# ScalarE's weight blocks in the attention steps: one ahead of the exponentials, the others at the end

## The chip, the cores and the metric

One core of a Trainium2 chip runs the whole program in one launch. The metric is the device time of a run in microseconds; of three runs of the kernel before, the median is 1616.29 us (1611.82 to 1618.34). PE is TensorE, PEld its weight load, DVE is VectorE, ACT ScalarE, POOL GpSimd, SP SyncE.

## What is computed

Three layers over 512 tokens of width 1024, in float32. Layer 0: windowed attention (8 heads, a window of 128, a learned sink) beside a multi-scale pooling, then an MLP. Layer 1: dense latent attention beside a gated recurrence, then an MLP. Layer 2: a short convolution, sparse attention with three branches (compressed, selected, window) and dilated attention with three dilations, then a gate. The two parts that the change touches compute, cut down:

```python
# layer 0 ("even")
s = where(|kpos - qpos| <= 128, q @ k.T * 64**-0.5, -inf)
m = maximum(max(s), sink); p = exp(s - m)
out = (p / (sum(p) + exp(sink - m))) @ v
x = x + concat([out, pooled(u)]) @ e_w_out
# layer 2 ("last")
u = rmsnorm(x) @ w_in_2          # 33 tiles of 128 columns
y_b = gate0 * softmax(q k_cmp) v_cmp + gate1 * softmax(q k_s) v_s + gate2 * softmax(q k_w) v_w
y_c = alpha_g * softmax(q k_dilated) v   # three groups
h = x + concat([y_a, y_b * silu(z), y_c * silu(z)]) @ w_out_2
```

## The kernel before

**Weights.** All weights come as one stream of 232 blocks, each 128x1024 (eight sub-blocks of 128x128). SP loads block b into slot b mod 4 of `raw`. The products are made with split numbers, three matmuls for one (L575, L576, L577): high by high, high by low, low by high. So each block is split on the chip: ACT copies it into its high half (`prepare`, L1048, in the MLPs L1143; semaphore `hi_made`), POOL subtracts to get the low half (L558, `lo_made`), and PE waits for `lo_made` before its first product with the block. `prepare(n)` makes all blocks up to n; for block b it waits for the load and for PE's last use of block b-4 (`acc_full` or `block_used`). POOL and SP run one loop over all blocks, each in the order of the stream.

**Attention.** Each of the three attentions (`attention("even", ...)`, `"mla"`, `"last"`) is a software pipeline over pairs of units (a unit is one head or branch on 128 queries). In step s PE makes the scores of pair s (L680), the values of pair s-3 (L698), the transposes of pair s-2 (L712), and then a fill: products of other work. DVE adds the mask and takes the minimum (L1555, out `negm`, semaphore `masked`), and scales the probabilities of pair s-1 (L1563, then L1569 or L1571, `p_ready`). ACT runs the exponentials of pair s (L1104) and copies the transposes of pair s-2 out of the bank (L1114, `pt_ready`). PE's scores of pair s+1 wait for `masked` of pair s, its values for `pt_ready`.

**Fills.** In the even attention (19 steps) the fill is four to six products a step of the remaining input tiles, the pooling map and the first part of the output map (`e_pace`, `E_BLOCKS`). In the last one (51 steps, numbered 0 to 50 here) it is the input projection: 12 products in steps 0 to 3, 10 in steps 4 to 11, then 4, from step 36 on 3 (`pace`, `Z_BLOCKS`). Some blocks of it are "parts" of the compression, used up by four matmuls at L946. DVE takes each finished tile out of its bank (L1886, L1884, in the even attention L1516, L1710, L1522) and runs what follows from it in `behind`, ahead of the next step's L1555: L1927 and L1932 (the dilated output by its share and by silu), L1861, L1624, L1628 (the short convolution), L1452 (low halves of the operands), in the even attention L1677 to L1692 (window sums) and L1530 to L1532 (rotations).

**ACT's order.** It is the order in which the code is written. In a step of the attentions:

```python
beside(step)              # copies and activations for tiles that the step before finished
exponentials(step)
turned_probs(step - 2)    # L1114
between(step)             # weight blocks
evacuate(k)               # at the end of a group
```

In the even and the last attention `between` makes the blocks whose slots the fill of the step before gave free; the one in the mla attention makes none. In the last attention steps 2 to 5, 8, 9 and 12 make two blocks, 6 and 7 three, 1, 10 and 11 one, and from step 14 on the steps 14, 16, ... 36 and 39, 42, 44 one each.

Of the kernel before, what the change touches and what calls it, by code (L numbers as in the profile page):

```python
# [37 lines left out]
RING = 4  # L38
# [202 lines left out]
def e_steps(n_steps):  # L241

    work, done, blocks, at = e_work(), [], [], 0
    ends = HEAD + E_AHEAD // SUBS
    for step in range(n_steps):
        events = []
        for stage, i, k in work[at:at + e_pace(step)]:
            count = {a: n for a, _, n in STAGES}[stage]
            sub = SUB0[stage] + i * count + k
            if k == count - 1:  # L250
                events.append((stage, i))
            ends += sub % SUBS == SUBS - 1 or (stage == "pool" and i == NTILES["pool"] - 1)
        at += e_pace(step)
        done.append(events)
        blocks.append(ends)
    assert at >= len(work), (at, len(work))
    return done, blocks
# [12 lines left out]
def z_steps(n_steps):  # L270

    work = [w for w in z_work(HEAD)] + [("out2", i, k) for i, k in OUT2_HEAD]
    done, blocks, at, ends = [], [], 0, HEAD
    for step in range(n_steps):
        names, left = [], pace(step)
        while at < len(work) and left:
            kind, n, what = work[at]
            at += 1
            if kind == "aside":
                names.append(what)  # L280
                continue
            left -= 1
            if kind == "product" and what == KT - 1:
                names.append(Z_HOSTS[n])
                ends += 1
            if kind == "part":
                ends += 1
                if what[1] == 3:
                    names.append(f"part{what[0]}")
        done.append(names)  # L290
        blocks.append(ends)
    assert at == len(work), (at, len(work))
    return done, blocks


def program(nc, x_t, stream, params, consts, ropes, p_t, out_t):
    with ExitStack() as ctx:
# [126 lines left out]
        E_DONE, E_BLOCKS = e_steps(len(EVEN) // 2 + VALUE_LAG)  # L424
# [16 lines left out]
        def z_banks():  # L441

            t0, held, out = TILE0["zin"], {}, {}
            for n in range(HEAD):
                out[Z_HOSTS[n]] = (4 + (t0 + n) % 4, None)
                held[4 + (t0 + n) % 4] = z_tile(Z_HOSTS[n])
            for n in range(HEAD, len(Z_HOSTS)):
                own, other = 6 + (n + 1) % 2, 6 + n % 2
                out[Z_HOSTS[n]] = (own, held.get(own))
                held[own] = z_tile(Z_HOSTS[n])  # L450
                for _, aside in Z_ASIDES.get(n, ()):
                    out[aside] = (other, held.get(other))
                    held[other] = z_tile(aside)
            return out, held
# [3 lines left out]
        Z_DONE, Z_BLOCKS = z_steps(len(LAST) // 2 + VALUE_LAG)  # L458
# [64 lines left out]
        def probs(i, n):  # L523

            return more[:, i % 4 - 2, 0:n] if i % 4 >= 2 else tmp[:, 2 + i % 4, 0:n]

        def groups_after(family, step):

            n = max(u["group"] for u in FAMILY[family]) + 1
            return [k for k in range(n) if last_of(family, k) // 2 + VALUE_LAG == step]  # L530
# [506 lines left out]
        def _(act):  # L1037
            prepared = [0]

            def prepare(n):  # L1040

                while prepared[0] <= min(n, NBLOCKS - 1):
                    b = prepared[0]
                    act.wait_ge(raw_in[b % RING], 16 * (b // RING + 1))
                    if b >= RING:
                        what, count = BLOCK_END[b - RING]
                        act.wait_ge(acc_full if what == "tile" else block_used, count)
                    nc.scalar.activation(w_hi[:, b % RING, :], raw[:, b % RING, :], ACT.Copy).then_inc(hi_made, 1)  # L1048
                    prepared[0] += 1
# [38 lines left out]
            def rows(stage):  # L1088
                return lambda m: act.wait_ge(z_ready, TILE0[stage] + m + 1)

            def attention(family, evacuate, beside=lambda step: None, between=lambda step: None):
                units, u0 = FAMILY[family], UNIT0[family]
                pairs = len(units) // 2

                def exponentials(p):
                    for i in (2 * p, 2 * p + 1):
                        u, gu = units[i], u0 + i
                        act.wait_ge(masked, gu + 1)
                        if u["sink"] is not None:
                            act.wait_ge(sink_put, gu + 1)  # L1100
                        if p >= 2:
                            act.wait_ge(pt_full, gu - 3)
                        w = u["n"] + (u["sink"] is not None)
                        nc.scalar.activation(probs(i, w), tmp[:, i % 2, 0:w], ACT.Exp, bias=negm[:, i:i + 1], scale=-1.0,  # L1104
                                             accum_out=den[:, i:i + 1]).then_inc(exp_done, 1)

                def turned_probs(p):
                    for i in (2 * p, 2 * p + 1):
                        u, gu = units[i], u0 + i
                        act.wait_ge(pt_full, gu + 1)  # L1110
                        if p:
                            act.wait_ge(pv_done, gu - 1)
                        w, m = (u["n"] + P - 1) // P * P, min(P, u["n"])
                        nc.scalar.activation(tmp[0:m, 4 + i % 2, 0:w], bank[4 + i % 2][0:m, 0:w],  # L1114
                                             ACT.Copy).then_inc(pt_ready, 1)

                for step in range(pairs + VALUE_LAG):
                    beside(step)
                    if step < pairs:
                        exponentials(step)  # L1120
                    if 0 <= step - TURN_LAG < pairs:
                        turned_probs(step - TURN_LAG)
                    between(step)
                    for k in groups_after(family, step):
                        evacuate(k)

# [92 lines left out]
                            act.wait_ge(z_ready, TILE0["pool"] + i + 1)  # L1219
                            hi_of("pooled", i, pooled_y[i])  # L1220

            def between_even(step):
                if step >= 1:
                    prepare(E_BLOCKS[step - 1] + RING - 1)

            def even_out(k):
                group_done("even", k)
                hi_of("eattn", k, bank[(GROUP0["even"] + k) % 2][:, :])

            attention("even", even_out, beside_even, between_even)  # L1230
            prepare(E_BLOCKS[-1] + RING - 1)
            act.dma_start(rope[:, :, :], ropes[1]).then_inc(rope_in, 16)

# [122 lines left out]
            block0 = SUB0["zin"] // SUBS  # L1356
# [43 lines left out]

            prepare(block0 + HEAD + RING - 1)

            def between_last(step):
                if step >= 1:
                    prepare(block0 + Z_BLOCKS[step - 1] + RING - 1)

            def last_out(k):
                if k >= 3:
# [2 lines left out]
                        act.wait_ge(acc_full, z_tile(1) + 1)  # L1411
                    hi_of(f"nsa{k - 3}", 0, z2(15 + k))

            attention("last", last_out, beside_last, between_last)
            act.wait_ge(p_in, 16)
            for k in range(2):
                nc.scalar.activation(mlp_op[:, 0, k, :], arena[:, 11 + k, :], ACT.Copy).then_inc(mlp_hi, 1)
# [747 lines left out]
```

## Time and profile before

| | |
|---|---|
| median of three runs | 1616.29 us (1611.82 to 1618.34) |
| the profiled execution | 1611.82 us, span 1610.0 us |
| mean granted clock of PE in it | 0.969 |
| PE busy | 1489.6 us, 93% |
| DVE, ACT, POOL busy | 783.1, 622.9, 566.1 us |
| even attention | about 44 to 161 us |
| last attention | about 1200 to 1509 us |

In the rows below a time is in us from the span's start. A row of a timeline has the start, the duration, the engine, the line, the operation, what it writes and reads, and how many alike were merged; in brackets stands how long the engine was idle before it and what ended that. A busy PE is not PE at its peak, since matmuls overlap. The granted clock is given as a share of 2.4 GHz.

### The profile page before, as it was taken

To read this page: it belongs to the slowest core of one execution; us is meant where nothing else is said; L and a number is where in the kernel's file an instruction comes from. 1 tells how busy PE (TensorE), PEld (TensorE's weight loads), DVE (VectorE), ACT (ScalarE), POOL (GpSimd) and SP (SyncE) were. 2 spreads that over 40 slices of the span, in tenths; PEclk is the share of its full clock that TensorE was granted. 3 is DMA by queue.
4 is the path that set the end of the run, shared out by engine and by line. 5 is a ranking of instruction groups with operands and counts; after the bars stand their busy time and mean duration, and the time that the engine had idled before them with its cause. 6 is when DMAs were issued, how large, how long until landed. Compare 5 with 4: busy or idle time off the path is not lost.

```text
span 1610.0 us, 20388 instructions
## 1 busy us (share of the span) xinstructions
PE 1489.6 (93%) x7110; PEld 1167.8 (73%) x7110; DVE 783.1 (49%) x1417; ACT 622.9 (39%) x1126; POOL 566.1 (35%) x236
## 2 busy tenths in 40 slices
PE   6979899999999987788999999999989799899997
PEld 5657678888888866545778888888867677666785
DVE  6783442223444677586333223444466236476434
ACT  4443332232323456545433232232353234655432
POOL 4222254444444433100235444444423352122441
PEclk9999999999999988979999999999989999899998
DMA  5212232322223221100123232332322232111221
GB/s 215 68 51 66 66 105 91 102 94 96 100 91 103 70 89 66 53 1 1 61 76 112 91 104 92 99 97 91 104 66 79 92 107 77 40 53 53 66 79 53
DMA packets 36624, 129.55 MB, mean 80 GB/s; under 512 B 4048, under 2 KB 4176, under 8 KB 36560
## 3 DMA queue, kind: packets, MB, share of 16 engines
q1 hardware_dynamic: 35136, 124.80, 23.7%
q10 hardware_dynamic: 1424, 3.90, 0.7%
q8 instruction: 40, 0.66, 0.2%
q14 instruction: 24, 0.20, 0.0%
HBM read 126.58 MB, written 2.10 MB: 80 GB/s over the span
## 4 chain that ended last, share of the span: by engine, by line
issue 58%; POOL 22%; PE 16%; DVE 2%; ACT 1%; POOLq 1%; DVEq 0%; ACTq 0%
POOL w L558 22%; PE bank L575 4%; PE bank L577 4%; PE bank L576 4%; PE bank L698 1%; PE bank L712 1%; PE bank L680 1%; DVE arena L1996 0%; POOLq L557 0%; POOLq L555 0%; ACT tmp L1114 0%; ACT tmp L1104 0%; DVE arena L1628 0%; DVE arena L1886 0%; ACT arena L1383 0%
## 5 line engine op out<-in xcount | busy, mean ns | idle before, releaser
L558 POOL TENSOR_TENSOR w<-raw,w 128x1024 fp32r<-128x1024 f32 x232 | 565.9, 2442 | 1010.8 <-ACT w L1048 628.2
L575 PE MATMUL bank<-opC,w 128*128 128x512 f32 x624 | 255.3, 409 | 26.0 <-POOL w L558 14.2
L577 PE MATMUL bank<-opC,w 128*128 128x512 f32 x624 | 246.8, 395 | 0.0
L576 PE MATMUL bank<-opC,w 128*128 128x512 f32 x624 | 246.4, 395 | 0.0
L1604 DVE TENSOR_TENSOR mlp_op<-arena,mlp_op 128x512 fp32r<-128x512 f32 x64 | 144.5, 2260 | 188.7 <-ACT mlp_op L1171 188.7
L575 PE MATMUL bank<-mlp_op,w 128*128 128x512 f32 x560 | 221.5, 396 | 10.0 <-DVE arena L1516 9.5
L1143 ACT ACTIVATE w<-raw 128x1024 fp32r<-128x1024 f32 x126 | 133.2, 1057 | 239.5 <-PE bank L577 239.5
L576 PE MATMUL bank<-mlp_op,w 128*128 128x512 f32 x560 | 220.5, 394 | 0.0
L577 PE MATMUL bank<-mlp_op,w 128*128 128x512 f32 x560 | 220.3, 393 | 0.0
L575 PE MATMUL bank<-opA,w 128*128 128x512 f32 x428 | 168.8, 394 | 6.8 <-ACT arena L1317 2.3
L577 PE MATMUL bank<-opA,w 128*128 128x512 f32 x428 | 167.4, 391 | 0.0
L576 PE MATMUL bank<-opA,w 128*128 128x512 f32 x428 | 167.2, 391 | 0.0
L575 PEld LDWEIGHTS bank<-opC,w 128*128 128x128 f32 x624 | 119.3, 191 | 55.9 <-issue 14.5
L1597 DVE TENSOR_TENSOR tmp<-tmp,rms 128x512 f32<-128x512 f32 x64 | 51.5, 805 | 210.9 <-ACT tmp L1151 210.5
L577 PEld LDWEIGHTS bank<-opC,w 128*128 128x128 f32 x624 | 119.0, 191 | 26.1
L576 PEld LDWEIGHTS bank<-opC,w 128*128 128x128 f32 x624 | 119.5, 191 | 23.0 <-issue 0.5
L575 PEld LDWEIGHTS bank<-mlp_op,w 128*128 128x128 f32 x560 | 106.7, 191 | 34.2 <-DVE arena L1516 11.0
L1151 ACT ACTIVATE tmp<-bank 128x512 f32<-128x512 f32 x64 | 38.3, 598 | 224.5 <-PE bank L577 213.9
L577 PEld LDWEIGHTS bank<-mlp_op,w 128*128 128x128 f32 x560 | 106.6, 190 | 22.5
L576 PEld LDWEIGHTS bank<-mlp_op,w 128*128 128x128 f32 x560 | 106.6, 190 | 22.2 <-issue 0.2
L1048 ACT ACTIVATE w<-raw 128x1024 fp32r<-128x1024 f32 x106 | 109.4, 1049 | 14.0 <-PE bank L577 13.2
L575 PEld LDWEIGHTS bank<-opA,w 128*128 128x128 f32 x428 | 80.6, 188 | 27.8 <-ACT arena L1317 5.6
(213 smaller groups left out, 1928.2 us busy)
## 6 DMA issues: line engine op xcount, KB each, us to landing
raw<-stream_dram SPq DMA_DIRECT2D x232, 512.0 KB, 3.4
out_t_dram<-arena SPq DMA_DIRECT2D x8, 256.0 KB, 2.1
x<-x_t_dram SPq DMA_DIRECT2D x4, 256.0 KB, 5.7
x<-x_t_dram ACTq DMA_DIRECT2D x4, 256.0 KB, 7.2
rope<-ropes_dram ACTq DMA_DIRECT2D x2, 512.0 KB, 6.8
con<-consts_dram ACTq DMA_DIRECT2D x1, 993.5 KB, 8.2
arena<-p_t_dram ACTq DMA_DIRECT2D x1, 512.0 KB, 4.2
par<-params_dram ACTq DMA_DIRECT2D x1, 253.5 KB, 3.8
```

The costliest lines, as they stand in the source:

```text
L558: pool.tensor_tensor(w_lo[:, j, :], raw[:, j, :], w_hi[:, j, :].bitcast(F32), ALU.subtract).then_inc(lo_made, 1)
L575: pe.matmul(out, wh, hi, start=first, stop=False)
L576: pe.matmul(out, wh, lo, start=False, stop=False)
L577: return pe.matmul(out, wl, hi, start=False, stop=last)
L680: pe.matmul(bank[2 + i % 2][:, 0:u["n"]], u["q"], u["k"], start=True, stop=True).then_inc(s_full, 1)
L698: mm = pe.matmul(into[at:at + 64, col:col + P], u["v"][b], tmp[0:kw, 4 + half, P * b:P * (b + 1)], start=(b == 0 and u.get("first", True)) ...
L712: mm = pe.transpose(bank[4 + i % 2][0:w, a:a + P], probs(i, SEQ)[:, a:a + w], ident)
L1048: nc.scalar.activation(w_hi[:, b % RING, :], raw[:, b % RING, :], ACT.Copy).then_inc(hi_made, 1)
L1143: nc.scalar.activation(w_hi[:, b % RING, :], raw[:, b % RING, :], ACT.Copy).then_inc(hi_made, 1)
L1151: nc.scalar.activation(tmp[:, j % 2, :], bank[4 + (t0 + j) % 4][:, :], ACT.Relu).then_inc(relu_made, 1)
L1597: TTn(tmp[:, j % 2, :], tmp[:, j % 2, :], rms[:, 1, :], ALU.mult).then_inc(vstep, 1)
L1604: TTn(mlp_op[:, 1, j % 2, :], u[:, bass.ds(SEQ * RING * i + SEQ * j, SEQ)], mlp_op[:, 0, j % 2, :].bitcast(F32), ALU.subtract).then_inc(ml ...
```

## The change

`attention` on ACT gets `blocks`, a function from the step to the number of the last block that may be made, in place of `between`. Ahead of the exponentials it makes blocks up to `min(blocks(step), prepared[0])`, which is one block if any is due; behind the copies it makes the rest. The functions of the two attentions return the numbers that they passed to `prepare` before; `-1` means none.

```diff
-            def attention(family, evacuate, beside=lambda step: None, between=lambda step: None):
+            def attention(family, evacuate, beside=lambda step: None, blocks=lambda step: -1):
...
                 for step in range(pairs + VALUE_LAG):
                     beside(step)
+                    prepare(min(blocks(step), prepared[0]))
                     if step < pairs:
                         exponentials(step)
                     if 0 <= step - TURN_LAG < pairs:
                         turned_probs(step - TURN_LAG)
-                    between(step)
+                    prepare(blocks(step))
                     for k in groups_after(family, step):
                         evacuate(k)
...
-            def between_even(step):
-                if step >= 1:
-                    prepare(E_BLOCKS[step - 1] + RING - 1)
+            def blocks_even(step):
+                return E_BLOCKS[step - 1] + RING - 1 if step else -1
...
-            def between_last(step):
-                if step >= 1:
-                    prepare(block0 + Z_BLOCKS[step - 1] + RING - 1)
+            def blocks_last(step):
+                return block0 + Z_BLOCKS[step - 1] + RING - 1 if step else -1
```

ACT in steps 5 and 6 of the last attention, before (w is a weight block's high half, raw_in the load of its slot, acc_full and block_used the release of the old block):

```order
L1048 ACTIVATE w<-raw 128x1024 [waits block_used,raw_in0]
L1104 ACTIVATE tmp,den<-tmp,negm 128x128 [waits pt_full,masked] x2
L1114 ACTIVATE tmp<-bank 128x128 [waits pv_done,pt_full] x2
L1048 ACTIVATE w<-raw 128x1024 [waits acc_full,raw_in1]
L1048 ACTIVATE w<-raw 128x1024 [waits acc_full,raw_in2]
L1048 ACTIVATE w<-raw 128x1024 [waits acc_full,raw_in3]
L1104 ACTIVATE more,den<-tmp,negm 128x128 [waits pt_full,masked] x2
```

and with the change:

```order
L1048 ACTIVATE w<-raw 128x1024 [waits block_used,raw_in0]
L1048 ACTIVATE w<-raw 128x1024 [waits acc_full,raw_in1]
L1104 ACTIVATE tmp,den<-tmp,negm 128x128 [waits pt_full,masked] x2
L1114 ACTIVATE tmp<-bank 128x128 [waits pv_done,pt_full] x2
L1048 ACTIVATE w<-raw 128x1024 [waits acc_full,raw_in2]
L1048 ACTIVATE w<-raw 128x1024 [waits acc_full,raw_in3]
L1048 ACTIVATE w<-raw 128x1024 [waits block_used,raw_in0]
L1104 ACTIVATE more,den<-tmp,negm 128x128 [waits pt_full,masked] x2
```

The first of step 6's three blocks (raw_in1) stands ahead of its exponentials, and the first of step 7's (raw_in0, the last but one row) ahead of step 7's.

ACT in step 24, before, from the Silu of six tiles on:

```order
L1383 ACTIVATE arena<-arena 128x512 [waits z_ready] x6
L1104 ACT_TABLE_LOAD [waits pt_full]
L1104 ACTIVATE tmp,den<-tmp,negm 128x31 [waits masked]
L1104 ACTIVATE tmp,den<-tmp,negm 128x31 [waits pt_full,masked]
L1114 ACTIVATE tmp<-bank 128x512 [waits pv_done,pt_full] x2
L1048 ACTIVATE w<-raw 128x1024 [waits acc_full,raw_in0]
```

and with the change:

```order
L1383 ACTIVATE arena<-arena 128x512 [waits z_ready] x6
L1048 ACTIVATE w<-raw 128x1024 [waits acc_full,raw_in0]
L1104 ACT_TABLE_LOAD [waits pt_full]
L1104 ACTIVATE tmp,den<-tmp,negm 128x31 [waits masked]
L1104 ACTIVATE tmp,den<-tmp,negm 128x31 [waits pt_full,masked]
L1114 ACTIVATE tmp<-bank 128x512 [waits pv_done,pt_full] x2
```

The step's only block moves from behind the copy of the transposes to ahead of the exponentials. The rows of PE, DVE, POOL and SP are the same in both kernels.

## Rows read from the trace of the kernel before

**Rows 1.** The page, busy time: us, share of the span, instructions.

```profile
PE 1489.6 (93%) x7110; PEld 1167.8 (73%) x7110; DVE 783.1 (49%) x1417; ACT 622.9 (39%) x1126; POOL 566.1 (35%) x236
```

**Rows 2.** PE's waits, 1195 to 1530: us in total, times, longest.

```profile
PE bank L575 <- POOL w L558: 12.2, 6, 4.3
PE bank L698 <- ACT tmp L1114: 10.3, 6, 7.3
...
PE bank L680 <- DVE negm L1555: 2.8, 3, 1.4
```

**Rows 3.** PE's waits, 44 to 172.

```profile
PE bank L575 <- DVE op_any L1452: 4.0, 2, 2.3
PE bank L680 <- DVE arena L1532: 2.7, 2, 2.2
```

**Rows 4.** Timeline of steps 5 and 6 of the last attention, PE, ACT, POOL.

```profile
1260.12 0.47 PE L575 MATMUL bank<-opC,w 128*128 128x512 f32 x1 [3.16 <-POOL w L558]
...
1268.27 0.40 ACT L1104 ACTIVATE tmp<-tmp,negm 128x128 f32<-128x128 f32 x1 [9.77 <-DVE negm L1555]
...
1270.49 6.99 POOL L558 TENSOR_TENSOR w<-raw,w 128x1024 fp32r<-128x1024 f32 x3 [8.09 <-ACT w L1048]
...
1272.99 0.76 PE L575 MATMUL bank<-opC,w 128*128 128x512 f32 x1 [4.26 <-POOL w L558]
```

**Rows 5.** Windows: us; busy PE, PEld, DVE, ACT, POOL; clock; DMA; GB/s.

```profile
1260.10:1263.10 3.00, 2.98 (x14) 2.47 (x15) 0.00 (x0) 0.00 (x0) 2.31 (x1) 1.00 0.50 175
1273.00:1278.70 5.70, 5.70 (x15) 4.54 (x16) 0.00 (x0) 0.00 (x0) 4.49 (x2) 0.50 0.61 192
1391.36:1401.60 10.24, 5.82 (x30) 5.01 (x31) 1.22 (x8) 7.24 (x17) 2.35 (x1) 0.50 0.13 31
```

**Rows 6.** Timeline, POOL and DVE, at 1369 and at 1487.

```profile
1369.46 2.39 POOL L558 TENSOR_TENSOR w<-raw,w 128x1024 fp32r<-128x1024 f32 x1 [9.01 <-ACT w L1048]
1369.86 2.60 DVE L1571 TENSOR_SCALAR tmp<-tmp,rden,gates 128x384 f32<-128x384 f32 x2
...
1487.00 0.87 DVE L1571 TENSOR_SCALAR more<-more,rden,gates 128x384 f32<-128x384 f32 x2
...
1489.14 3.38 POOL L558 TENSOR_TENSOR w<-raw,w 128x1024 fp32r<-128x1024 f32 x1 [8.34 <-ACT w L1048]
```

**Rows 7.** Timeline of step 28, DVE and PE's next scores.

```profile
1411.79 0.69 DVE L1886 TENSOR_TENSOR arena<-bank,rms 128x512 f32<-128x512 f32 x1 [0.68 <-PE bank L577]
1412.39 1.89 DVE L1932 TENSOR_TENSOR arena<-arena 128x512 f32<-128x512 f32 x3
...
1415.48 0.08 DVE L1555 DVE_READ_ACCUMULATOR2_ANT negm<- 128x1 f32 x1
...
1415.80 0.49 PE L680 MATMUL bank<-arena 64*128 64x256 f32 x2
```

**Rows 8.** Timeline of steps 26, 34 and 39, DVE and PE's next scores.

```profile
1404.02 1.89 DVE L1927 TENSOR_TENSOR arena<-arena 128x512 f32<-128x512 f32 x3
...
1438.71 0.69 DVE L1886 TENSOR_TENSOR arena<-bank,rms 128x512 f32<-128x512 f32 x1 [1.47 <-PE bank L577]
...
1440.17 0.55 DVE L1624 TENSOR_SCALAR arena<-arena,par 128x512 f32<-128x512 f32 x1
...
1445.49 0.70 PE L680 MATMUL bank<-arena 64*128 64x512 f32 x2 [1.38 <-DVE negm L1555]
...
1467.31 0.49 PE L680 MATMUL bank<-arena 64*128 64x256 f32 x2 [0.79 <-DVE negm L1555]
```

**Rows 9.** Timeline behind steps 24, 30 and 44, ACT and PE.

```profile
1395.62 1.05 ACT L1048 ACTIVATE w<-raw 128x1024 fp32r<-128x1024 f32 x1
...
1395.78 0.48 PE L698 MATMUL bank<-tmp,arena 128*64 128x128 f32 x2 [7.33 <-ACT tmp L1114]
...
1425.85 0.33 PE L698 MATMUL bank<-tmp,arena 128*64 128x128 f32 x2 [0.69 <-ACT tmp L1114]
...
1488.16 0.32 PE L698 MATMUL bank<-tmp,cmpv 31*64 31x128 f32 x2 [0.81 <-ACT tmp L1114]
```

More of the change, by code:

```diff
@@ L1228, in even_out @@
                 hi_of("eattn", k, bank[(GROUP0["even"] + k) % 2][:, :])
-            attention("even", even_out, beside_even, between_even)
+            attention("even", even_out, beside_even, blocks_even)
             prepare(E_BLOCKS[-1] + RING - 1)
@@ L1412, in last_out @@
                     hi_of(f"nsa{k - 3}", 0, z2(15 + k))
-            attention("last", last_out, beside_last, between_last)
+            attention("last", last_out, beside_last, blocks_last)
             act.wait_ge(p_in, 16)
```

## The prediction

> **What bounds the kernel now.** I read the page first: PE is busy 93% of the span [rows 1], so a change on ScalarE (ACT) only counts where PE waits. The change touches ACT's order in two attentions, so I then asked who ended PE's waits there. In the last attention (steps 0 to 50, from 1200 us) the largest entry is POOL: six waits of a product at L575 for the low half of a weight block, 12.2 us in all. Behind it stand six waits for ACT's copy L1114, 10.3 us, 7.3 of them one wait, and three for the minimum `negm` that DVE makes in L1555, 2.8 us [rows 2]. In the even attention PE never waits for POOL; it waits for DVE, 4.0 us for L1452 and 2.7 for L1532 above all [rows 3]. So a weight block that comes earlier can gain in the last attention alone.
>
> Step 6 shows where POOL's waits come from [rows 4]. ACT sat idle for 9.77 us before the exponentials at 1268.27, and made its three blocks only behind them and the two copies. POOL, idle for 8.09 us, began on them at 1270.49, and the product that needs the first of them started at 1272.99 after 4.26 us of waiting. The slot's old block had long been used up: the release of the first block of steps 2 to 7 lies in the middle or the beginning of the fill before. The block was late because of ACT's order alone.
>
> **The early steps (1 to 13), where the change gives.** The first block moves ahead of the exponentials, into ACT's idle time: its 1.05 us (the one at 1395.62) [rows 9] fit into 9.77. In steps 2 to 6 this is the block PE waited for, and it comes several us sooner, more than the 0.67 to 4.26 us of any wait. In step 7 PE waited for the second of three; POOL then has one less before it, 2.4 us against a wait of 0.7. The second and third blocks stay where they were and find POOL freer. I take all six waits as gone: **-12.2 us**. Bounds: 0 if the time came back at once as another wait, 12.2 if not; DVE and ACT are idle for most of these steps, so the upper end.
>
> The wait of 4.26 us also cost clock. PE worked for 5.70 us at a granted clock of 0.50 (1.2 GHz) right behind it, where behind the 3.16 us wait of the step before [rows 4] the clock was 1.00 (2.4 GHz) [rows 5]. At full clock this work takes 2.85 us: **-2.8 us**. Bounds 0 and -2.85.
>
> **The late steps, where the change takes.** From step 12 a step has only four, later three, products, and 15 steps make one block (14 to 36 even, 39, 42, 44). PE waits for POOL in none of them, so nothing can be gained. Two things move.
>
> First, ACT: the block takes 1.05 us ahead of the exponentials. The block is released when the last product of the step before ends, about when the scores start; normally ACT then waits over a microsecond for DVE's `negm` or PE's transposes before it can start the exponentials, and that covers the block. The cover is missing where ACT itself is late: in step 24 behind six Silu, in step 30 behind two Silu and three copies, in step 44 behind two copies. There PE waited 7.33, 0.69 and 0.81 us for the copy L1114 [rows 9]; in step 24 the block stands behind the copy before the change (it starts at 1395.62, and PE at 1395.78), ahead of it after. Three times 1.05: **+3.2 us**. Bounds 0 and 3.2.
>
> Second, POOL and DVE. POOL's 2.4 us start right behind the block, so they move from behind ACT's copies to about 1.2 us after the start of the scores, on top of DVE's work. What that costs the trace shows: two L1571 on 384 columns take 0.87 us alone, but 2.60 us when they start at 1369.86, inside POOL's 1369.46 to 1371.85; they end 0.6 us behind POOL [rows 6]. A DVE operation that has started goes on; the next one that reads and writes SBUF alone waits for POOL's end. Operations that read a bank, L1555 and L1886, are not held. The Trainium skill says the same (GPSIMD Engine Reference, § 8 Key points: it shares its SBUF interfaces with VectorE, with contention against instructions in a two-port mode or with two SBUF inputs). This rule speaks against the change, and the trace agrees: by it the sum below is -4.0, without it -11.8.
>
> In most late steps the operations held are the scalings L1571, needed a step later, and behind them DVE waits for PE's next scores anyway: nothing. In four steps DVE has other work on SBUF ahead of L1555, and PE or ACT waits for L1555:
> - Step 28: L1886 starts at 1411.79, right behind the last product, then come three L1932 and one L1452, then `negm`, done at 1415.56, and PE starts the next scores at 1415.80 [rows 7]. The block would be ready at 1412.9 and POOL run to 1415.3. The first L1932 gets through, the second waits from 1413.0 on: 2.3 us later, of which 0.2 are slack and 0.2 come back as a wait for the copy. +2.3.
> - Step 34: POOL would run 1439.9 to 1442.3, L1624 wait from 1440.17: 2.1 later. PE waited 1.38 us for `negm` already [rows 8]. +2.1.
> - Step 39: the same row of operations, PE waited 0.79 us already [rows 8]. +2.0.
> - Step 26: three L1927 from 1404.02 [rows 8] would wait 2.3, but PE's next scores are at 1407.85, 1.5 us behind `negm`; the rest returns as a wait for the copy. +1.5.
>
> Sum **+7.9 us**. Bounds: 0 if DVE's back-to-back operations kept POOL out, 9.2 (four times 2.3) if nothing were slack. I take the value worked out, since rows 6 show a second operation held.
>
> **The even attention.** Five products to a step, and the same hold. Two POOL runs that now lie on DVE's pooling chains leave them (about 1.3 us of PE's waits go), step 10's moves onto its L1452 and L1710 (+2.4 us), step 11's off its L1452 (-1.5), and ACT is later by some tenths twice. These come from placing each block by hand in the timeline, as for step 28. Net 0; bounds -3 and +3, less than half of the waits in rows 3 either way.
>
> **Sum.** -12.2 - 2.8 + 3.2 + 7.9 + 0 = -3.9 us. The profiled execution took 1611.8 us (span 1610.0 and 1.8 around it) and would take 1607.9. It was the fastest of three; against their median of 1616.3 the forecast is **1612.4 us**, 0.24% less. A difference of 0.5% is 8.1 us, about what a measurement of this kernel can tell from none. Everything else keeps its order: PE, DVE, POOL and the DMA queues run the same list, loads only follow POOL earlier, and no table load is added.
>
> **Rivals.**
> - *DVE isn't held where it hurts* (its back-to-back operations keep the way, or POOL starts some tenths later than I place it and falls behind them). For it: POOL took 3.38 us at 1489.14, beside DVE's L1452, so sometimes POOL gives way [rows 6]. Against it: rows 6. The 7.9 fall away: 1616.3 - 11.8 = 1604.5. Chance 0.24.
> - *The clock falls in the late steps.* Place: the waits behind steps 28, 34 and 39, which grow to 2.3, 3.5 and 2.8 us. The clock fell at the waits of 4.26 and 7.33 us and not at 3.16 [rows 4, 5, 9], so this decides from somewhere above 3.2 us on, or lower where several waits lie close. A fall costs half of 5.70 or 5.82 us of PE work [rows 5], 2.9; three cost 8.6: 1612.4 + 8.6 = 1621.0, slower than before. For it: these steps have small matmuls and waits between them. Against it: only one of the three waits exceeds 3.2. Chance 0.12.
> - *Nothing comes of it*: PE reaches its next wait sooner and stays there as long, or gain and loss both fail to show. Against it: ACT and POOL idle for 8 to 10 us before step 6's blocks [rows 4]. 1616.3. Chance 0.08.
> - The forecast, both halves as worked out: 0.56, with its own range 1608 to 1617.
>
> **Numbers.** Faster by over 0.5% (under 1608.2): most of the first rival, 0.20, and the forecast's lower edge, 0.07. Slower by over 0.5% (over 1624.4): a third of the second rival and edges, 0.06. Within 0.5%: 0.67. The range that leaves out 2 in 10 takes in both rivals' middles: 1604 to 1621.
>
> **What would show it.** PE's waits for POOL at L575 in the last attention gone, ACT's block ahead of the exponentials at step 6, clock 1.00 around it. PE's wait behind step 24 at 8.4 instead of 7.33. DVE's L1932, L1624 and L1927 rows lengthened by about 2.3 us with POOL beside them, PE's wait for `negm` behind step 34 near 3.5. If those DVE rows keep their length, my late loss is wrong and the kernel is faster than forecast; if POOL waits remain early, the gain is wrong; if PE's clock shows a new half-speed stretch after 1405 us, the second rival holds.

## The result, and the profile after

The changed kernel took **1619.8 us** (median of 20 runs, 1618.95 to 1622.33), the kernel before in the same comparison 1615.8 (20 runs, 1611.51 to 1620.47). The ratio is 1.0028, 95% interval 1.0021 to 1.0035: some 4 us slower, where 3.9 us less was forecast. That is about a quarter of a percent, but the sign is the other one, and the interval leaves no room for a gain.

The profiled execution has a span of 1618.7 us at a mean granted clock of 0.962, the one of before 1610.0 at 0.969. The latter was among the fastest of its kernel, so the two profiles stand 8.7 us apart where the medians stand 4.0. From the page, busy time (us, share of the span, instructions); it answers to [rows 1]:

```profile
PE 1498.7 (93%) x7110; PEld 1173.3 (72%) x7110; DVE 791.3 (49%) x1417; ACT 625.3 (39%) x1126; POOL 567.8 (35%) x236
```

The work is the same, instruction for instruction; PE's is 9 us longer, which no matmul added: that is clock. DVE's is 8 us longer: operations that were held.

PE's waits from 1195 to 1530 (us in total, times, longest), against [rows 2]. DVE's lines are one lower in the changed kernel than before (L1931 here is L1932 there), and up to eight higher in the kernels further down; L1048, L1104, L1114 and most of PE's are the same:

```profile
PE bank L698 <- ACT tmp L1114: 14.3, 7, 8.3
PE bank L680 <- DVE negm L1554: 7.4, 5, 3.3
...
PE bank L698 <- DVE arena L1949: 2.7, 2, 2.5
```

All six waits for POOL, 12.2 us, are gone. The waits for ACT's copy grew from 10.3 to 14.3, those for `negm` from 2.8 to 7.4, and one for DVE's copy of a finished group, 2.5, stands at step 7, where the trace of before had 0.78. Net: -12.2 + 4.0 + 4.6 + 1.7 = -1.9 us. PE's waits in the even attention (44 to 175) sum to 12.7 us against 12.9 before, in other places:

```profile
PE bank L575 <- DVE arena L1709: 3.6, 1, 3.6
PE bank L657 <- DVE op_any L1451: 2.6, 1, 2.6
PE bank L575 <- DVE op_any L1451: 2.3, 1, 2.3
PE bank L680 <- DVE arena L1531: 2.2, 1, 2.2
PE bank L698 <- ACT tmp L1114: 1.5, 1, 1.5
```

So by its waits the changed kernel should be about 2 us faster. What it lost is, as the next rows show, in the clock. Windows of its late steps; columns as in [rows 5], the third number from the right is the clock:

```profile
1403.10:1406.52 3.42, 3.42 (x10) 2.59 (x8) 0.00 (x0) 0.47 (x4) 0.00 (x0) 0.50 0.00 0
1413.34:1416.76 3.42, 3.20 (x14) 2.01 (x11) 1.79 (x9) 2.21 (x11) 0.00 (x0) 0.50 0.15 61
1447.47:1450.89 3.42, 3.25 (x19) 1.88 (x16) 2.37 (x8) 1.37 (x5) 0.00 (x0) 0.50 0.01 2
1471.37:1478.19 6.82, 6.12 (x19) 3.93 (x19) 2.34 (x8) 2.06 (x11) 2.15 (x1) 0.50 0.23 77
1495.26:1498.67 3.41, 3.38 (x14) 2.76 (x15) 2.80 (x5) 1.53 (x6) 0.99 (x1) 0.50 0.36 102
```

Five stretches at 1.2 GHz between steps 27 and 47, with 19.4 us of PE work in them; in the profile of before the clock is 1.00 from the end of the stretch of [rows 5] (1401.60) to 1599. At full clock this work takes half: some 9.7 us.

**Reading waits and clock apart.** Each run lists its span S and mean granted clock c. S x (1 - c) is what the reduced clock would cost if PE were busy throughout; call it the *clock loss*, and the rest of the time the *rest*. The loss counts stretches in which PE waits anyway, so only its differences between kernels are used; means over the runs of a kernel, c has three digits (0.001 is 1.6 us for one run). By the spread of the runs, twice the standard error of such a difference is 0.9 to 2.9 us for the clock loss and 0.5 to 1.3 us for the rest. The changed kernel: loss 61.9, rest 1558.2. The kernel before, in the three sets of experiments below that have most runs of it (21, 17 and 35): loss 52.2, 53.2, 53.6, rest 1562.5, 1562.1, 1562.1. So the change took **4.0 us off the rest and added 8.3 to 9.7 us of clock loss**.

### The profile page after: what moved, and what is told of

Its sections match the earlier page's. It is cut to its first block, busy times and chain, and to the rows that moved or that the text cites. A ratio compares the mean times of both kernels' runs of the same rounds, so it can differ in the third digit from the quotient of the medians.

```text
span 1618.7 us, 20388 instructions
## 1 busy us (share of the span) xinstructions
PE 1498.7 (93%) x7110; PEld 1173.3 (72%) x7110; DVE 791.3 (49%) x1417; ACT 625.3 (39%) x1126; POOL 567.8 (35%) x236
## 4 chain that ended last, share of the span: by engine, by line
PE 80%; DVE 12%; ACT 5%; issue 3%; POOL 0%; DVEq 0%; ACTq 0%; POOLq 0%
PE bank L575 23%; PE bank L577 23%; PE bank L576 23%; PE bank L698 3%; PE bank L680 3%; PE bank L712 3%; DVE arena L1627 1%; ACT tmp L1114 1%; PE bank L657 1%; PE bank L644 1%; DVE arena L1515 1%; ACT tmp L1104 1%; DVE tmp L1554 1%; DVE arena L1751 1%; DVE rms L1478 1%
## 5 line engine op out<-in xcount | busy, mean ns | idle before, releaser
L1048 ACT ACTIVATE w<-raw 128x1024 fp32r<-128x1024 f32 x106 | 110.0, 1050 | 47.7 <-PE bank L577 46.9
```

## Experiments

Theory at this point: (a) the early steps give about 15 us as forecast, less 2.4 at step 7; (b) in the late steps POOL's earlier block holds DVE operations on SBUF, and ACT is late by its own block, 8.2 us; (c) behind these longer waits the clock falls, which costs as much again. Rivals: the clock falls because the blocks move at all, or because of the even attention; the DVE operations are long for another reason.

### The change in parts

Three kernels make the early call in some steps only; the condition on `family` and `step` is all that differs:

```diff
-                    prepare(min(blocks(step), prepared[0]))
+                    if family == "last" and step in range(14):
+                        prepare(min(blocks(step), prepared[0]))
```

**Steps 0 to 13 of the last attention alone.**

> The block stands ahead of the exponentials only in steps 0 to 13 of the last attention; everywhere else the order is the one before. Theory (the change gains in the early steps and loses in the late ones, by holds and by falls of PE's clock): the early part gave 15.4 us and took 2.4 back at step 7 in the profile after, so -13 us against the kernel before, 1603. No wait of PE for POOL in the last attention, no half-speed stretch between the one behind step 24 and the end of the attention. Rival (the early gain is an accident of where the clock fell in one profiled run): -9 us or less, since then only the 12.2 us of waits less 2.4 are real. Second rival (gain and loss are coupled, the early gain only shifts later work into a worse place): about 0.

Measured: 1601.56 us, 0.9929 of before (0.9911 to 0.9947). **Steps 14 to 50 alone** (`range(14, 51)`):

> The block stands ahead only from step 14 of the last attention on. Theory with the clock: steps 25 to 46 lose 16.7 us in the profile after, so about +16 us, 1632, and three or more new half-speed stretches behind step 26. Rival (waits alone, the clock stretches being chance): +8 us, the sum of the longer waits of PE (0.95 + 1.3 + 1.9 + 0.9 + 1.4 + 0.9 + 0.9), 1624.

Measured: 1631.76 us, 1.0107 (1.0088 to 1.0126); rest +6.7, clock loss +10.1. **The even attention alone:**

> The block stands ahead only in the even attention. Theory: holds shift between DVE's pooling chains and cost 1.5 us in the profile after: +1.5 us, 1617, the wait for L1710 at step 10 at 3.6 instead of 1.5 us and that for the second L1452 of step 11 shorter. Rival (no effect beyond noise): within 0.5 us of the kernel before.

Measured: 1617.06 us, 1.0014 (1.0004 to 1.0025); rest +0.4, clock loss +1.8.

The parts add up: -12.2 + 16.8 + 2.4 (differences of means) = +7.0, the whole measured +4.5; the intervals of the three are wide enough for that. The change is a gain of 12 us and a loss of 19 us under one line of code, and of the loss 12 us are clock. PE's waits from 1185 to 1525 in the kernel with the early steps alone show the gain and its leak:

```profile
PE bank L698 <- ACT tmp L1114: 10.3, 6, 7.3
...
PE bank L680 <- DVE negm L1555: 2.8, 3, 1.4
...
PE bank L698 <- DVE arena L1950: 2.7, 2, 2.5
```

ACT's and `negm`'s are as in [rows 2], POOL's entry is absent, DVE's copy is at 2.7.

### Does POOL hold DVE in the late steps?

The changed kernel, but in late steps the early block's signal to POOL is given only behind the step's copies. ACT works as early as in the change, POOL as late as before.

```diff
+                    if owed[0]:
+                        nc.scalar.activation(unread[:, 0:1], c("ones"), ACT.Copy).then_inc(hi_made, 1)
+                        owed[0] = 0
                     prepare(blocks(step))
```

> The changed kernel, but from step 14 of the last attention on the early block's hi_made is raised by a small activation behind the copies of the transposes, so that ACT still makes the block ahead of the exponentials and POOL starts where it did before the change (0.2 us more of ACT in 15 steps). Theory (POOL's run holds DVE's operations in SBUF): the rows of L1926 at step 26, L1931 at step 28 and L1623 at step 34 are as short as before the change (1.9, 1.9 and 0.6 us), PE's wait for negm behind step 34 is 1.4 again, the waits for the copy behind 24, 30, 40 and 44 stay, 0.9 us longer each or some more; the time is 1619.8 - 4 to - 8 = 1612 to 1616. Rival (ACT's own delay is what costs): no change against the changed kernel, 1620, with the long waits for negm still there.

Measured: 1609.42 us, 0.9974 (0.9964 to 0.9984). Against the changed kernel that is 0.0054 or 8.7 us less by the ratios (10.4 by the medians, which come from two comparisons). Timelines of step 28, first the changed kernel, then this one:

```profile
1406.91 0.69 DVE L1885 TENSOR_TENSOR arena<-bank,rms 128x512 f32<-128x512 f32 x1 [4.00 <-PE bank L577]
1406.97 1.06 ACT L1048 ACTIVATE w<-raw 128x1024 fp32r<-128x1024 f32 x1 [3.40 <-PE bank L577]
1407.52 4.08 DVE L1931 TENSOR_TENSOR arena<-arena 128x512 f32<-128x512 f32 x3
1408.11 2.95 POOL L558 TENSOR_TENSOR w<-raw,w 128x1024 fp32r<-128x1024 f32 x1 [8.42 <-ACT w L1048]
...
1412.94 0.88 PE L680 MATMUL bank<-arena 64*128 64x256 f32 x4 [1.95 <-DVE negm L1554]
```

```profile
1403.11 1.89 DVE L1940 TENSOR_TENSOR arena<-arena 128x512 f32<-128x512 f32 x3
...
1407.29 0.19 ACT L1131 ACTIVATE unread<-con 128x1 f32<-128x1 f32 x1
1407.56 2.40 POOL L558 TENSOR_TENSOR w<-raw,w 128x1024 fp32r<-128x1024 f32 x1 [6.94 <-ACT unread L1131]
```

The same three products take 4.08 us with POOL beside them and 1.89 without; the first two take 0.68 us each, and the third, which starts behind POOL, 2.88:

```profile
1408.72 2.88 DVE L1931 TENSOR_TENSOR arena<-arena 128x512 f32<-128x512 f32 x1
```

PE's waits for `negm` are back at 2.8 us, those for ACT's copy stay at 14.0. The hold is shown, and its price with it: against before, rest -7.8 and clock loss +2.8, where the change has -4.0 and +8.3 to +9.7. So taking the hold away gave back 3.8 us of rest and 5.5 to 6.9 us of clock.

### The hold that was missed, at step 7

Steps 0 to 13 alone again, and in step 7 the early block waits for the tile that DVE evicts just ahead of its product on `x`:

```diff
+                        if family == "last" and step == 7:
+                            act.wait_ge(z_ready, z_tile(Z_DONE[6][-1]) + 1)
                         prepare(min(blocks(step), prepared[0]))
```

> The early block in steps 0 to 13 of the last attention alone, and in step 7 that block also waits for the tile whose eviction stands ahead of the product of x (L1900 there), so that GpSimd's third block starts behind that product and not ahead of it. Theory (a running GpSimd block holds a VectorE operation whose operands are all in SBUF): the product takes 0.75 us instead of 2.4, the copy of group 0 comes 1.7 us earlier, TensorE's wait for it falls from 2.45 us to 0.8 as in the kernel before; 1.6 us below the kernel with the early steps alone (0.9929 of before), so 0.9919 of before, about 1601. Rival (the copy of group 0 from the bank is itself late for another reason, or TensorE is only held back one product later because the third block's rest is now late): the wait for the copy stays at 2.45 or a wait for L558 of about 1 us takes its place, 0.993 of before.

Measured: 1600.45 us, **0.9913** (0.9900 to 0.9926). The timeline with the early steps alone, then with the wait:

```profile
1262.18 7.15 POOL L558 TENSOR_TENSOR w<-raw,w 128x1024 fp32r<-128x1024 f32 x3 [4.70 <-ACT w L1048]
...
1267.46 2.42 DVE L1900 SCALAR_TENSOR_TENSOR x<-x,par,rms 128x512 f32<-128x512 f32 x1
1269.80 0.68 DVE L1950 COPY arena<-bank 128x512 f32<-128x512 f32 x1
...
1270.63 0.44 PE L698 MATMUL bank<-tmp,arena 128*64 128x128 f32 x4 [2.45 <-DVE arena L1950]
```

```profile
1269.74 0.74 DVE L1902 SCALAR_TENSOR_TENSOR x<-x,par,rms 128x512 f32<-128x512 f32 x1
1269.85 1.06 ACT L1048 ACTIVATE w<-raw 128x1024 fp32r<-128x1024 f32 x1 [4.53 <-DVE arena L1888]
1270.39 0.68 DVE L1952 COPY arena<-bank 128x512 f32<-128x512 f32 x1
1270.99 2.39 POOL L558 TENSOR_TENSOR w<-raw,w 128x1024 fp32r<-128x1024 f32 x1 [1.79 <-ACT w L1048]
...
1271.22 0.44 PE L698 MATMUL bank<-tmp,arena 128*64 128x128 f32 x4 [0.78 <-DVE arena L1952]
```

POOL's third block starts behind the product on `x`, which takes 0.74 instead of 2.42 us, and the wait falls from 2.45 to 0.78, as expected; no wait for POOL takes its place. The clock of that profile is 1.00 there:

```profile
1268.00:1290.00 22.00, 21.22 (x110) 16.90 (x108) 9.64 (x30) 9.84 (x25) 15.47 (x7) 1.00 0.54 169
```

In the four other profiles with early blocks in the early steps the wait is 2.45 us and the clock falls 1.1 to 1.2 us behind it. That is also where the gain shows over the runs: the rest is the same with and without the mend (-12.1 and -12.4 against before), though the wait is 1.7 us shorter, and the clock loss goes from +0.1 to -2.4, each good to 2 or 3 us. So the shorter operation and the shorter wait are shown; what the mend is worth in time is not. This is the fastest kernel of the study, 14 us below the one before by the ratio, and the difference of its ratio to that with the early steps alone has the expected sign, though the two intervals overlap.

### Which late steps cost, and what

**The early steps and eight late ones in which no wait grew** (14, 16, 18, 20, 22, 32, 36, 42):

> The early block in steps 0 to 13 and in steps 14, 16, 18, 20, 22, 32, 36 and 42, in none of which TensorE waited longer in the changed kernel's profile. Theory (a late step costs only where it makes TensorE wait longer or makes the clock fall behind such a wait): as with steps 0 to 13 alone, 0.993 of before, 1603 to 1604. Rival (the clock falls because the blocks are moved at all, whatever TensorE waits): three of the five new half-clock stretches come back, 3 x 1.7 = 5 us more, 0.996.

Measured: 1606.5 us, 0.9948 (0.9931 to 0.9964); rest -11.6, clock loss +1.9. PE's waits are, entry by entry, those of the early steps alone. The ratio lies between the two expectations and its interval takes in most of both. Against the early steps alone it is 3 us more, and with both intervals -1 to 7 us: inconclusive.

**Steps 24, 30, 39 and 44 alone, ACT's part:**

> The early block in steps 24, 30, 39 and 44 alone, where it puts ScalarE's exponentials or copies 1 us later. Waits of TensorE for L1114 grow by 0.95 us each, 3.8 us in sum. If waits alone count: 1.0024 of before, +3.8 us. If each longer wait can also make the clock fall for 3.4 us (a loss of 1.7 us each): up to 3.8 + 4 x 1.7 = 10.6 us, 1.0066. If neither (what is lost is made up before the next due point): 1.000.

Measured: 1618.54 us, 1.0021 (1.0010 to 1.0033); rest +3.6, clock loss -0.3. The waits for L1114 are 14.1 us instead of 10.3, and the time grew by no more than that. The clock did not fall behind them: its profile has no stretch at 0.50 from 1403.5 to 1604. One window of it:

```profile
1429.00:1450.00 21.00, 19.38 (x114) 13.31 (x114) 13.26 (x39) 7.86 (x25) 2.40 (x2) 1.00 0.15 51
```

**Steps 26, 28 and 34 alone, POOL's part:**

> The early block in steps 26, 28 and 34 alone, where GpSimd then runs while VectorE has operations with both operands in SBUF. TensorE's waits for negm grow by 1.3 us behind step 26, 1.95 at step 28 and 1.94 at step 34: 5.2 us, 1.0032 of before, if waits alone count; with a clock stretch of 1.7 us behind each up to 10.3 us, 1.0064. Rival (the holds cost nothing by themselves): 1.000.

Measured: 1625.04 us, 1.0070 (1.0057 to 1.0083); rest +5.9, clock loss +4.6. The waits grew by 5.4 us (`negm` 2.8 to 7.4, L1114 10.3 to 11.1). Step 34 and the clock behind it:

```profile
1448.72 2.46 POOL L558 TENSOR_TENSOR w<-raw,w 128x1024 fp32r<-128x1024 f32 x1 [3.27 <-ACT w L1048]
1448.98 2.48 DVE L1624 TENSOR_SCALAR arena<-arena,par 128x512 f32<-128x512 f32 x1
...
1456.24 1.13 PE L680 MATMUL bank<-arena 64*128 64x512 f32 x4 [3.32 <-DVE negm L1555]
```

```profile
1456.24:1457.75 1.51, 1.13 (x4) 0.30 (x4) 0.80 (x5) 1.51 (x6) 0.00 (x0) 1.00 0.00 0
1457.75:1461.16 3.41, 3.22 (x18) 2.57 (x19) 2.19 (x8) 1.36 (x4) 0.00 (x0) 0.50 0.01 2
```

L1624 takes 2.48 us where it took 0.55 [rows 8], PE waits 3.32 us, and 1.5 us after the wait the clock drops. **One of the three at a time:**

> The early block in step 28 alone, so that GpSimd holds the three products of L1932. TensorE then waits 1.95 us longer for negm at the next scores: 1.0012 of before (1.95 us) if the wait alone counts. The three steps 26, 28 and 34 together cost 11 us where their waits grew by 5.4: if each hold can make the clock fall behind it, about a third of the rest here, 4 us, 1.0023.

> The early block in step 34 alone, so that GpSimd holds L1624. TensorE waits 1.94 us longer for negm: 1.0012 of before if the wait alone counts; with a clock stretch behind it (1.5 us; the one late stretch of the run with all three lay 4 us behind this step's scores) 1.0021 or more.

> The early block in step 26 alone, so that GpSimd holds the three products of L1927. TensorE waits 1.3 us more in two pieces (0.7 and 0.7): 1.0008 of before if the waits alone count. If the rest of the 11 us of steps 26, 28 and 34 comes from holds whatever their wait, 1.002.

Measured: step 28 1.0030 (1.0018 to 1.0043), rest +1.9, clock loss +3.2; step 34 1.0025 (1.0010 to 1.0041), rest +1.8, loss +2.8; step 26 1.0012 (0.9999 to 1.0025), rest +1.4, loss +0.5. The rest grows by each step's own wait (1.95, 1.94, 1.3), and behind 28 and 34 the clock costs about as much again or more (3.2 and 2.8, each good to 1.5 or 1.7 us); behind 26, whose wait comes in two pieces of 0.7, it costs little (0.5, good to 1.4). With step 28 alone the profile has the clock down 0.9 us behind its wait:

```profile
1420.40 0.70 PE L680 MATMUL bank<-arena 64*128 64x256 f32 x4 [1.95 <-DVE negm L1555]
1421.28:1424.69 3.41, 3.18 (x11) 2.35 (x12) 1.59 (x8) 2.20 (x9) 0.00 (x0) 0.50 0.07 25
```

### Is it the wait that lowers the clock, or POOL's and ACT's earlier work?

The kernel before, with three more products of 128x512 on DVE at those places, on a tile nobody reads; no block moves.

```diff
+            def spend():
+                for i in range(3):
+                    step(TTn(spare[:, :], rms[:, 0, :], rms[:, 0, :], ALU.mult))
```

> The kernel before, no block moved, with three more 128x512 products on VectorE (a spare tile, not read) behind each of the three places that GpSimd held in steps 26, 28 and 34: 3 x 0.73 = 2.2 us each, so that negm is as late as with the early blocks, and GpSimd, ScalarE and the transfers as in the kernel before. Theory (the loss is TensorE's longer waits and the clock that falls behind them): as with steps 26, 28 and 34 alone, 1.007 of before, 11 us. Rival (the waits cost themselves only, and the rest comes from GpSimd, ScalarE or the transfers running earlier): 5.4 us, 1.0033.

Measured: 1.0028 (1.0014 to 1.0042). The products of the second place stood in step 25 and not in step 28, where PE made the time up: the waits grew by 2.8 us (`negm` +4.7, ACT's copy -1.9), not 5.4, rest +3.6, clock loss +1.3. The load stood in the wrong step, so this kernel doesn't decide the question. Once more, placed:

> As e12_vector_load, with the three spare products behind the three places that GpSimd held (L1927 in step 26, L1932 in step 28, L1624 in step 34) and not in step 25: no block moved, negm late by 2.2 us in each, TensorE's waits longer by 1.3, 1.95 and 2.2 us, 5.4 in sum. Theory (the clock falls behind TensorE's longer waits, whoever makes them): the loss to the clock grows as with the early blocks in steps 26, 28 and 34, by 4.6 us in the mean, about +10 us, 1.006. Rival (GpSimd's or ScalarE's earlier block takes part in the clock's fall): the clock's loss stays within 1 us of the kernel before, +5.4 us, 1.0033.

Measured: 1621.28 us, 1.0041 (1.0027 to 1.0055), between the two expectations; rest +5.1, clock loss +2.1. Step 34 there, and its clock:

```profile
1455.27 1.13 PE L681 MATMUL bank<-arena 64*128 64x512 f32 x4 [3.56 <-DVE negm L1556]
```

```profile
1456.90:1460.32 3.42, 3.36 (x18) 2.71 (x19) 3.42 (x7) 2.32 (x6) 2.36 (x1) 0.50 0.00 0
```

With POOL and ACT as in the kernel before, the clock falls at the same place behind the same wait. All kept profiles say so of step 34: in nine its wait is 3.3 or 3.6 us, five times by POOL's hold and four times by DVE's own load, and in all nine the clock falls 0.3 to 2.0 us behind it; in nine the wait is 1.4 us, and in one of them the clock falls there. Behind step 28's wait of 1.9 us it fell in two of five profiles with the hold and in none of three with the load. Whether it does so as often was still open, since the 1.0070 and the 1.0041 came from two chips. Both again on one chip, with a third kernel that has DVE's extra products and ACT's block early, POOL's late:

> The kernel of e6_late_pool once more, on one chip with e16_vector_load_same_chip: together with it, it tells whether the 1.0070 and the 1.0041 of two calls are two numbers or one. If GpSimd's and ScalarE's earlier blocks take part in the clock's fall: 4 us (0.0025) above the kernel with the load on VectorE. If the longer waits do all of it: the same ratio within 0.001, both near 1.0055.

> The kernel of e13_vector_load_placed once more, on one chip with e15_late_pool_same_chip. Waits alone, with the clock falling behind them: near 1.0055 as e15. Otherwise 1.0035 to 1.0045, and e15 at 1.0065 or more.

> The three spare products on VectorE as in e13_vector_load_placed, and in the same steps 26, 28 and 34 ScalarE makes its block early, but GpSimd gets it only behind the copies of the step, as before. If ScalarE's earlier block takes part in the clock's fall: at e15's ratio. If GpSimd's earlier block does, or neither: at e16's ratio.

Measured: 1.0051 (1.0039 to 1.0064) with POOL's hold, 1.0045 (1.0032 to 1.0058) with DVE's own load, 1.0054 (1.0035 to 1.0073) with ACT early as well; clock loss +4.2, +2.1, +3.1, rest +4.5, +4.9, +4.9. The first two differ by 0.0006 (interval -0.0012 to 0.0024), nearer to what was expected if the wait alone does it than to the 0.0025 of the rival, though neither kernel came out at the value expected for it (1.0055 for both, or 1.0035 to 1.0045 and 1.0065). The third decides nothing, since its interval takes in both others. Shown is that the wait lowers the clock without any block moved: the two kernels with DVE's load have each +2.1 us of clock loss, good to 1.7 and 1.1. Whether POOL's or ACT's earlier block adds to that stays open. The clock losses say it may: +4.6 and +4.2 with POOL's hold, some 2 us more than with the load, for the same sum of waits.

In the table, the number in brackets is twice the standard error of the clock loss.

| early block in | waits by the trace, us | rest | clock loss |
|---|---|---|---|
| all (the change) | -1.9 | -4.0 | +8.3 to +9.7 |
| last, 0 to 13 | -10.5 | -12.4 | +0.1 (2.9) |
| the same, step 7 mended | -12.2 | -12.1 | -2.4 (1.6) |
| last, 14 to 50 | +8.6 | +6.7 | +10.1 (1.9) |
| all, POOL held back late | -6.8 | -7.8 | +2.8 (0.9) |
| 24, 30, 39, 44 | +3.8 | +3.6 | -0.3 (1.5) |
| 26, 28, 34 | +5.4 | +5.9 | +4.6 (1.7) |
| 28 / 34 / 26 alone | +1.95 / +1.94 / +1.3 | +1.9 / +1.8 / +1.4 | +3.2 (1.5) / +2.8 (1.7) / +0.5 (1.4) |
| none, DVE load at 26, 28, 34 | +5.5 | +5.1 | +2.1 (1.7) |

The rest follows the sum of PE's waits within 2.1 us, in seven of the eleven cases within 0.6. The clock loss doesn't follow that sum.

## Why the prediction was wrong

**The early steps: right, but for step 7.** The waits for POOL were taken as gone, -12.2, and are. The clock term of -2.8 came in the profile only as far as step 6 goes: from 1249 to 1275 the changed kernel has clock 1.00:

```profile
1249.00:1275.00 26.00, 24.24 (x131) 19.67 (x129) 13.12 (x28) 8.31 (x19) 17.07 (x7) 1.00 0.37 122
```

In its place the fall came behind the longer wait of step 7 (1276.81 to 1280.22 in the changed kernel), and over the runs of the kernel with the early steps alone nothing of the -2.8 is left (+0.1); with step 7 mended it is -2.4. Missed was the hold at step 7. The prediction looked for SBUF operations ahead of `negm`, in the late steps only; here the held one stands ahead of DVE's copy of group 0, for which PE waits as well. A term of +2.4 by the timeline, +1.7 in the wait alone; the kernel with step 7 mended shows the hold and the wait.

**ACT's late term: right in kind, mis-sized.** +3.2 was forecast, three times 1.05. The waits for L1114 grew by 3.8, four times 0.95. The fourth is step 39, which the prediction had put down to DVE. There ACT's conversion L1058 of the step before stands ahead of the block and itself waits 4.58 us for DVE; the block is made at 1470.05, its POOL run falls behind DVE's work, and instead the copy is late:

```profile
1469.51 0.63 ACT L1058 ACTIVATE op_any<-arena 128x512 fp32r<-128x512 f32 x1 [4.58 <-DVE arena L1952]
1469.74 0.70 PE L680 MATMUL bank<-arena 64*128 64x256 f32 x4 [0.78 <-DVE negm L1554]
1470.05 1.04 ACT L1048 ACTIVATE w<-raw 128x1024 fp32r<-128x1024 f32 x1
...
1472.07 0.69 PE L698 MATMUL bank<-tmp,arena 128*64 128x128 f32 x4 [1.62 <-ACT tmp L1114]
```

**POOL holding DVE: right at three steps of four.** Forecast +2.3, +2.1, +2.0, +1.5 for steps 28, 34, 39, 26. Measured in the waits 1.95, 1.94, 0 and 1.3, together 5.2 instead of 7.9. The prediction had the first product of step 28 get through and the second held; it was the third that was held (2.88 us), and DVE came out late by nearly as much. It took rows 6 for a second operation held; of the two L1571 there it is the first that took long:

```profile
1369.86 2.21 DVE L1571 TENSOR_SCALAR tmp<-tmp,rden,gates 128x384 f32<-128x384 f32 x1
```

The first rival (DVE not held, 0.24) fell. By the Trainium skill (GPSIMD Engine Reference, § 8 Key points) GpSimd contends with VectorE instructions that have two SBUF inputs, which spoke against the change. The products of L1931 are such instructions, and their 4.08 us against 1.89 agree with it. (The -4.0 that the prediction gives for the sum by this rule is its -3.9.)

**The even attention: right in its waits.** Net 0 was forecast, 12.9 went to 12.7. Step 10's wait for L1709 grew from 1.5 to 3.6 as placed. The clock cost 1.8 us there, which had no term.

**The clock in the late steps: the step that failed.** The four terms that are waits, corrected, are -12.2 + 1.7 + 3.8 + 5.2 = -1.5 (-1.9 by the entries above, where a small wait fell away), and by them alone the kernel would be faster, as forecast. The prediction gave the late clock its second rival (1621.0, 0.12; measured 1619.8) and set it aside with "only one of the three waits exceeds 3.2". That threshold was read from three waits of one profile [rows 4, 5, 9], one fall at 4.26, one at 7.33 and none at 3.16, and it doesn't hold: with step 28 alone, whose wait is 1.95 us, the clock loss grew by 3.2 us. It doesn't even hold for the waits it was read from. The wait of 3.16 us at step 5 stands unchanged in 13 of the kept profiles, and in two of them the clock falls 1.5 us behind it; in four more it falls 1.0 us behind step 4's wait of 2.49. One of the two, from the kernel with steps 26, 28 and 34:

```profile
1265.09 0.47 PE L575 MATMUL bank<-opC,w 128*128 128x512 f32 x1 [3.16 <-POOL w L558]
1266.60:1270.02 3.42, 3.42 (x12) 2.76 (x11) 0.00 (x0) 0.00 (x0) 0.76 (x1) 0.50 0.72 238
```

So whether a wait of 2 to 3 us is followed by a fall differs from one execution to the next; the term needs a chance, not a limit. The prediction's own sign for this rival, a half-speed stretch after 1405 us, came four times. The rival's own words allowed for it ("or lower where several waits lie close"), and the chance should have followed them, not the threshold. It also named the price as 2.9 us a fall; in the changed kernel's profile four stretches cost 1.6 to 1.7 us each (half of the 3.2 to 3.4 us of PE work in them) and one 3.1. That the rival's 1621.0 lies near the measured time is in part luck: three falls at 2.9 stand for five shorter ones.

What stays open: why ACT's four longer waits (3.8 us) cost no clock by themselves, loss -0.3, and POOL's three (5.4 us) did; no run separates their size from their place. Nor is it certain that ACT's are free: the kernel with POOL held back has ACT's four as its only longer late waits, and its loss is +2.8, with a fall at 1463.17, right behind one of 1.62 us. And falls come without a longer wait too: with the early steps alone one stands at 1456.18, behind waits of 0.8 and 0.7 us that are as long as before, where the profile of before has none:

```profile
1456.18:1459.59 3.41, 3.41 (x9) 2.19 (x7) 0.24 (x2) 1.27 (x6) 2.46 (x1) 0.50 0.00 0
```

A single profile draws one case of several; the means over runs decide.

## What to carry to other kernels

An engine's idle time is room for that engine alone: before moving its work there, follow what the work sets off (here POOL's pass on the same block) and look for operations of VectorE on SBUF under it, ahead of anything TensorE waits for, copies of results as well as the minimum. Where a region has no wait for the thing that is made earlier, leave its order alone; the same move gave 12 us in the first fourteen steps of the last attention and cost 17 in the rest of it. And give TensorE's clock a term with a chance wherever a wait grows in a region of small matmuls, even by 2 us, and set no limit from one profile: read the loss from every run's span and granted clock.

## What the runs showed of the hardware

- The clock was granted at 0.50 behind waits far shorter than the 4.26 us at which the trace of before had it: in the mean it cost 3.2 us for a wait that grew to 1.95, and 2.8 for one that grew by 1.94 (to 3.32).
- The same wait is followed by a fall in one execution and not in the next: behind 3.16 us the clock was 1.00 in eleven profiles and 0.50 in two, behind 1.9 us it fell in two of eight, behind 3.3 to 3.6 us at step 34 in nine of nine.
- A longer wait lowered the clock with either engine behind it: with VectorE's own load and no block moved the clock loss grew by 2.1 us in both comparisons. POOL's hold, with the same waits, gave 4.6 and 4.2; whether POOL or ScalarE adds to it is not shown.
- The same kernel in two comparisons on two chips gave 1.0070 (1.0057 to 1.0083) and 1.0051 (1.0039 to 1.0064); the intervals overlap, so a difference between chips isn't shown, but a single ratio of such a kernel is no steadier than that.
- A VectorE operation with operands in SBUF that starts behind POOL's block is held to about its end: 0.74 to 2.42 us, 0.55 to 2.48, and 0.68 to 2.88 for the third product of step 28, while the two before it kept their 0.68. POOL's block is longer beside them in part: 2.95 us against 2.40 in step 28, 2.46 in step 34.
